# Spreading the triangular-solve level steps of a fused two-layer trunk over twelve half jobs instead of eight, with the gate, key and value jobs behind it reordered

## The chip, the cores and the metric

One core of a Trainium2 chip runs the whole program. The metric is the device time of one execution in microseconds, the median of three runs. TensorE multiplies; VectorE (DVE), ScalarE (ACT) and GpSimd (POOL) do elementwise work; SyncE's queue (SP) issues the weight transfers.

## The reference, cut to what matters

For x of 256 tokens by 1024 channels, two layers of: an RMSNorm, one wide projection (q, k, v, z, decay and beta logits, latents, gates), a gated delta rule over chunks of 64, latent attention, gating, an output projection, and a feed-forward block.

```python
qkv_a = jax.nn.silu(_causal_conv(qkv_a, conv_w[l]))
lower = jnp.where(strict, kk, 0.0) + jnp.eye(CHUNK, dtype=kk.dtype)
sol = lax.linalg.triangular_solve(lower, rhs, left_side=True, lower=True, unit_diagonal=True)
...
o_a = _rms_norm(o_a, gdn_norm_w[l]) * jax.nn.silu(z_a.reshape(b, s, GDN_HEADS, GDN_DV))
y_a = o_a.reshape(b, s, GDN_HEADS * GDN_DV) @ w_branch_a[l]
...
h = gates[:, :, 0] * y_a + gates[:, :, 1] * y_b
x = x + _rms_norm(h @ w_out[l], post_mix_norm_w[l])
```

## The kernel before

**Jobs and pieces.** All large products are cut into jobs. A job yields 256 output channels by 256 tokens in one of three PSUM banks (job j uses bank j mod 3, and waits for the evacuation of job j - 3). Its weights come in pieces of 128 x 1024 floats. Each piece is loaded by one 512 KB transfer that SP issues, then ScalarE writes its rounded upper part (whi, line 1110 through split_hi) and VectorE the remainder (wlo, line 1455, split_lo), and TensorE forms three products for each pair of 128x128 blocks: whi by upper, whi by lower, wlo by upper activations (lines 610 to 612). A piece is 24 such matmuls ("dense products"), each with its own weight load. The ring holds four pieces, so a piece is split three pieces ahead, and never before the piece four back is used up. "kn" and "vt" jobs (keys and values projected up from the latent) use half a piece each, "uq" jobs (queries) one piece of 768 columns, most others two. ScalarE evacuates k, v, q, z, gate, kn, vt and uq jobs.

**The order.** There is no runtime scheduler. `schedule()` (lines 121 to 268) writes out one list, ORDER, of (step, number). Every engine walks the same list and does its part of each step, with semaphore waits between engines; so each engine's queue is in that order, and an engine that waits in a step holds up all steps behind it. "half" is a job's first piece, "job" the rest; "late" steps are put behind the next job. `jobs_of_a_layer()` (lines 67 to 85) numbers the pieces in the order of use, which is also the order in memory and of SP's transfers.

**The level steps.** The triangular systems are solved by doubling: four levels (blocks of 2, 4, 8, 16), each with lvP and lvV (lines 899 to 924). Each of the two is 64 tiny products of 32 rows, which run as 128 matmuls with 128 weight loads: two halves of 64 pairs, a "burst" each. lvP of a level waits for VectorE's transpose of the level before (lv_xt); VectorE multiplies its result by a mask into PBq (line 1693, lv_p_out); lvV waits for that; VectorE then subtracts it from Xq and transposes (lines 1699, 1701). In before, a step's first half stands ahead of half a job and its second half inside it, behind six dense products (k == 1 of that piece), through the table LEVEL_STEP and `second_part`; 18 dense products follow. The eight steps lie on the eight pieces of v 0, v 1, (gate 0), v 2 and v 3. At the fifth step (n == 4) one half of gate 0 comes ahead of the step, and its other half takes the second part:

```python
for n, (kind, part, i) in enumerate(between):
    if steps[n][0][0] in ("lvP", "lvV"):
        LEVEL_STEP[...] = steps[n][0]
    o.extend(steps[n])
    part(kind, i)
    o.extend(behind[n])
```

**Behind the levels.** pairP, pairV, lastP, lastV, and t_v0, t_st, t_ks, t_v1 finish the solve and the chunk recurrence, one in front of each half of the q jobs. conv and silu (lines 1567, 1248) are the causal convolution on VectorE, six instructions a job, and its SiLU on ScalarE. Then come the kn jobs, qk 0 and 1 (TensorE at 878, evacuated by VectorE at 1672), kr (the shared rotary key: TensorE 851, VectorE 1623 to 1634), t_o (outputs of the delta rule: TensorE 1007, copied to oT by ScalarE 1371), the vt jobs and the uq jobs. ScalarE's evacuation of vt 0 waits for kr_out (line 1238), because the buffers overlap. t_o half h waits for qk_out 2 + 2h.

**The output norms.** For pair i of heads: osq i is a Square of oT on ScalarE (line 1281), then POOL adds the scaled square of q (line 1919, signal on_sq); onrm i is a product with a matrix of ones on TensorE that waits for on_sq i + 1 (lines 1019 to 1025, signal on_mm), then Ln and Exp on ScalarE (lines 1125 and 1127), a multiplication on VectorE (1723); osplit applies z on POOL and splits. In before, the rounds of the uq loop are: uq 4, osq 1; uq 5, (rope), onrm 0, osq 2; uq 0, (rope), onrm 1, osq 3; uq 1, onrm 2; uq 2, onrm 3; uq 3; then the attention scores sc 0. osq 0 is ahead of uq 4.

Of the kernel before, what the change touches and what calls it, by code (L numbers as in the profile page):

```python
# [66 lines left out]
def jobs_of_a_layer():  # L67


    jobs, n = [], 0  # L70
    for kind, numbers, pieces in (("lat", range(3), 2), ("k", range(1), 2), ("z", range(1), 2), ("k", range(1, 4), 2),
                                  ("z", range(1, 4), 2), ("v", range(2), 2), ("gate", range(1), 2), ("v", range(2, 4), 2),
                                  ("q", range(4), 2),
                                  ("kn", range(4), 0.5), ("vt", range(4), 0.5), ("uq", (4, 5, 0, 1, 2, 3), 1),
                                  ("gate", range(1, 8), 2), ("ya", range(4), 2), ("yb", range(4), 2),
                                  ("out", range(4), 2), ("ff1", range(16), 2), ("ff2", range(4), 8)):
        for i in numbers:
            jobs.append((kind, i, list(range(int(n), max(int(n) + 1, int(n + pieces))))))
            n += pieces
    for j, (kind, i, pieces) in enumerate(jobs):  # L80
        if kind in ("lat", "ff1") and i == 0:
            p = pieces[0]
            jobs[j] = (kind, 0, [p, p + 2])
            jobs[j + 1] = (kind, 1, [p + 1, p + 3])
    return jobs, int(n)
# [35 lines left out]
def schedule():  # L121
# [49 lines left out]
    half("z", 3)  # L171
    job("z", 3)

    between = [(kind, part, i) for kind in "vq" for i in range(4) for part in (half, job)]
    behind = {n: [] for n in range(len(between) + 3)}
    for n in range(8):
        behind[2 * n + 2].append(("conv", 4 + n))
        behind[2 * n + 3].append(("silu", 4 + n))
    for i in range(4):
        behind[2 * i + 5].append(("zsilu", i))  # L180
    behind[0].append(("latm", 0))
# [7 lines left out]
    steps = [[(step, lv)] for lv in range(len(SIZES)) for step in ("lvP", "lvV")]  # L189
    steps += [[(step, 0)] for step in ("pairP", "pairV", "lastP", "lastV")]  # L190
    steps += [[(step, 0), (step, 1)] for step in ("t_v0", "t_st", "t_ks", "t_v1")]
    for n, (kind, part, i) in enumerate(between):
        if steps[n][0][0] in ("lvP", "lvV"):
            LEVEL_STEP[JOBS[JOB["gate", 0]][2][1] if n == 4 else JOBS[JOB[kind, i]][2][n % 2]] = steps[n][0]
        if n == 4:
            half("gate", 0)
        o.extend(steps[n])
        if n == 4:
            job("gate", 0)
        part(kind, i)  # L200
        o.extend(behind[n])
    job("kn", 0)
    o += behind[16] + [("q2", 0)]
    job("kn", 1)
    o += [("qk", 0), ("qk", 1), ("qd", 0), ("kr", 0)]
    job("kn", 2)
    o += behind[17]
    job("kn", 3)
    o += [("q2", 1), ("q2", 2), ("q2", 3), ("lnexp", 1), ("t_o", 0)]
    job("vt", 0)  # L210
    o += [("qk", 2), ("qk", 3), ("qd", 1)]
    job("vt", 1)
    job("vt", 2)
    o.append(("t_o", 1))
    job("vt", 3)
    o.append(("osq", 0))
    for n, i in enumerate((4, 5, 0, 1, 2, 3)):
        job("uq", i)
        if i >= 4:
            late.append(("qrope", i - 4))  # L220
        if 1 <= n <= 4:
            o.append(("onrm", n - 1))
        if n < 3:
            o.append(("osq", n + 1))
    o += [("exptanh", 0), ("sc", 0), ("osplit", 0), ("osplit", 1)]
    for n in range(6):
        job("gate", 1 + n)
# [47 lines left out]
def build(nc, x_in, pos_in, w_in, prm_in, cst_in, out):  # L275
    with ExitStack() as ctx:
# [291 lines left out]
        def _(pe):  # L568
# [356 lines left out]

            def second_part(l, n, k):

                if n in LEVEL_STEP and k == 1:
                    step, lv = LEVEL_STEP[n]
                    (lvP_part if step == "lvP" else lvV_part)(l, lv, (2, 3))  # L930

            def pairP(l, _):
# [165 lines left out]
                      sc=sc, tr=tr, pv=pv, ysum=ysum, qrope=qrope)  # L1098
            for l in range(DEPTH):
                for what, n in ORDER:  # L1100
                    if what in do:
                        do[what](l, n)


# [945 lines left out]
```

How the kernel before makes its waits and increments, by code:

```python
        @block.sync  # L543
        def _(sp):
            def x_part(c):
                sp.dma_start(xT[:, 2 * c:2 * c + 2, :], x_in[:, 2 * c:2 * c + 2, :]).then_inc(s_x[c], 16)
            for n in range(DEPTH * NPIECE):
                if n == 2:
                    x_part(2)
                    x_part(3)
                elif n < 2:
                    x_part(n)
                sp.wait_ge(lo_ready, n + 1)
                sp.dma_start(raw[n % RING][:], w_in[n]).then_inc(loaded[n % RING], 16)
                if n == RING - 1:
                    sp.dma_start(cst[:, 0:C_FREQ], cst_in[:, 0:C_FREQ]).then_inc(s_in, 16)
                    sp.dma_start(pos_i[:], pos_in).then_inc(s_tab, 16)
                    sp.dma_start(cst[:, C_FREQ:NCST], cst_in[:, C_FREQ:NCST]).then_inc(s_tab, 16)
            for c in range(4):
                pair = slice(2 * c, 2 * c + 2)
                sp.wait_ge(x_done, due(DEPTH, x_done, 2 * c + 2))
                sp.dma_start(out[:, pair, :], xT[:, pair, :]).then_inc(s_out, 16)
            sp.wait_ge(s_out, 4 * 16)
# [2 lines left out]
        @block.tensor  # L567
        def _(pe):
            mm = nc.tensor.matmul
            pe.sem_inc(steps_done, RING)
            pe.wait_ge(s_warm, 1)
            for _n in range(8):
                mm(side[4][:, 0:S], sq[0][:, 0:P], sq[0][:, 0:S], start=True, stop=True)
# [9 lines left out]
            def piece(l, n):  # L584
                pe.wait_ge(lo_ready, l * NPIECE + n + 1 + RING)
                return whi[n % RING], wlo[n % RING]
```

## Time and profile before

| what | value |
|---|---|
| time, median of 3 runs | 1038.16 us (1035.57 to 1040.65) |
| profiled execution, its own time | 1044.89 us |
| span of the profiled execution | 1043.1 us |
| mean granted TensorE clock | 0.992 |
| TensorE busy (matmul) | 98% of the span |
| VectorE, ScalarE, POOL busy | 70%, 54%, 10% |
| weights | 304 transfers of 512 KB, 3.9 us to landing |

A time in the trace counts from the start of the span. Layer 0's level steps lie at about 84 to 133 us, layer 1's at 598 to 649 us. In a timeline a row is one instruction or a run of like ones (x with their number), the bracket is the idle time ahead of it and what ended it; "issue" there means that the profile shows nothing that was waited for. A granted clock of 1.00 is 2.4 GHz and of 0.50 is 1.2 GHz.

### The profile page before, as it was taken

Reading aid. Unit: us, or ns where it says so; the run is one execution under the profiler, and the core shown is the slowest. Engines: PE = TensorE matmul, PEld = TensorE weight load, DVE = VectorE, ACT = ScalarE, POOL = GpSimd, SP = SyncE. Lnnn points to the kernel's source line nnn. Section 1 sums busy time; section 2 is a strip of 40 time slices with the busy share of each in tenths; the row PEclk is TensorE's granted clock in tenths of the full one; section 3 lists DMA queues with packets and bytes.
Section 4 is the critical chain, followed back from the end, with each engine's and each line's share of the span. In section 5 each row is a group of like instructions: output and inputs, shape, how many; then the busy total and the mean of one; then the engine's idle time right before and its main releaser. Section 6 shows DMA issues by size and latency. Waiting matters only on the chain.

```text
span 1043.1 us, 24322 instructions
## 1 busy us (share of the span) xinstructions
PE 1019.8 (98%) x10626; PEld 990.7 (95%) x10626; DVE 733.4 (70%) x1024; ACT 558.7 (54%) x791; POOL 100.0 (10%) x76
## 2 busy tenths in 40 slices
PE   9998999999999999999999989999999999999996
PEld 8998999899999999999999989998999999999995
DVE  7887568697576788654598665677865777885543
ACT  7675475746445544434466634767554445544441
POOL 0010001310000222100000100015000003221000
PEclk9999999999999999999999989999999999999998
DMA  8543433434565466666535444334356646666661
GB/s 293 163 138 127 122 98 109 122 125 166 174 188 178 136 202 190 202 198 188 179 112 172 121 124 124 104 120 126 100 181 183 185 137 188 197 189 200 197 182 41
DMA packets 45609, 163.86 MB, mean 157 GB/s; under 512 B 5184, under 2 KB 5440, under 8 KB 45504
## 3 DMA queue, kind: packets, MB, share of 16 engines
q1 hardware_dynamic: 45360, 162.16, 50.4%
q8 instruction: 84, 1.38, 0.5%
q14 instruction: 21, 0.17, 0.1%
q10 hardware_dynamic: 144, 0.15, 0.0%
HBM read 161.25 MB, written 1.05 MB: 156 GB/s over the span
## 4 chain that ended last, share of the span: by engine, by line
PE 88%; DVE 7%; issue 2%; ACT 2%; DMA 0%; SPq 0%; DVEq 0%; ACTq 0%
PE dense L610 23%; PE dense L611 22%; PE dense L612 22%; DVE wlo L1455 2%; PE sides L922 1%; PE sides L1075 1%; PE sides L1049 1%; PE sides L1050 1%; PE sides L910 1%; PE dense L593 1%; PE dense L594 1%; PE sides L594 1%; PE sides L593 1%; PE dense L595 1%; PE sides L595 1%
## 5 line engine op out<-in xcount | busy, mean ns | idle before, releaser
L1455 DVE TENSOR_TENSOR wlo<-raw,whi 128x1024 fp32r<-128x1024 f32 (+1 forms) x303 | 392.6, 1303 | 196.9 <-ACT whi L1110 196.4
L1110 ACT ACTIVATE whi<-raw 128x1024 fp32r<-128x1024 f32 (+2 forms) x305 | 316.0, 1044 | 222.3 <-PE dense L612 201.6
L610 PE MATMUL dense<-uh,whi 128*128 128x256 f32 x768 | 224.8, 293 | 2.7 <-DVE ul L1484 1.3
L611 PE MATMUL dense<-ul,whi 128*128 128x256 f32 x768 | 215.3, 280 | 0.0
L612 PE MATMUL dense<-uh,wlo 128*128 128x256 f32 x768 | 215.1, 280 | 0.0
L610 PEld LDWEIGHTS dense<-uh,whi 128*128 128x128 f32 x768 | 146.6, 191 | 5.1 <-DVE ul L1484 1.4
L611 PEld LDWEIGHTS dense<-ul,whi 128*128 128x128 f32 x768 | 146.0, 190 | 1.3 <-issue 1.0
L612 PEld LDWEIGHTS dense<-uh,wlo 128*128 128x128 f32 x768 | 146.0, 190 | 0.0
L610 PE MATMUL dense<-fuh,whi 128*128 128x256 f32 x512 | 142.8, 279 | 0.4 <-DVE ful L1827 0.4
L611 PE MATMUL dense<-ful,whi 128*128 128x256 f32 x512 | 141.9, 277 | 0.0
L612 PE MATMUL dense<-fuh,wlo 128*128 128x256 f32 x512 | 141.9, 277 | 0.0
L610 PE MATMUL dense<-fh,whi 128*128 128x256 f32 x384 | 106.0, 276 | 0.0
L611 PE MATMUL dense<-fl,whi 128*128 128x256 f32 x384 | 106.0, 276 | 0.0
L612 PE MATMUL dense<-fh,wlo 128*128 128x256 f32 x384 | 106.0, 276 | 0.0
L610 PEld LDWEIGHTS dense<-fuh,whi 128*128 128x128 f32 x512 | 96.2, 188 | 1.6 <-issue 1.1
L612 PEld LDWEIGHTS dense<-fuh,wlo 128*128 128x128 f32 x512 | 96.4, 188 | 0.0
L611 PEld LDWEIGHTS dense<-ful,whi 128*128 128x128 f32 x512 | 96.1, 188 | 0.1
L610 PEld LDWEIGHTS dense<-fh,whi 128*128 128x128 f32 x384 | 72.1, 188 | 0.0
L611 PEld LDWEIGHTS dense<-fl,whi 128*128 128x128 f32 x384 | 72.1, 188 | 0.0
L612 PEld LDWEIGHTS dense<-fh,wlo 128*128 128x128 f32 x384 | 72.1, 188 | 0.0
L1929 POOL TENSOR_TENSOR fr<-fr 128x512 f32<-128x512 f32 x32 | 44.9, 1405 | 118.5 <-DVE fr L1796 118.5
L1899 POOL TENSOR_TENSOR sq<-sq,sq 128x512 f32<-128x512 f32 x8 | 10.4, 1296 | 349.9 <-ACT sq L1246 349.9
(320 smaller groups left out, 2095.5 us busy)
## 6 DMA issues: line engine op xcount, KB each, us to landing
raw<-weights SPq DMA_DIRECT2D x304, 512.0 KB, 3.9
xT<-x_t SPq DMA_DIRECT2D x4, 256.0 KB, 5.3
out_t<-xT SPq DMA_DIRECT2D x4, 256.0 KB, 2.3
cst<-consts SPq DMA_DIRECT2D x1, 512.0 KB, 8.1
prm_all<-params ACTq DMA_DIRECT2D x1, 150.0 KB, 3.8
pos_i<-pos SPq DMA_DIRECT2D x1, 128.0 KB, 7.8
cst<-consts SPq DMA_DIRECT2D x1, 6.0 KB, 7.6
```

What stands on the lines that cost most here:

```text
L593: mm(o_, h_[:, ws], ahi[:, k0 + k, :], start=first and k == 0, stop=False, skip_group_check=True)
L594: mm(o_, h_[:, ws], alo[:, k0 + k, :], start=False, stop=False, skip_group_check=True)
L595: x_ = mm(o_, l_[:, ws], ahi[:, k0 + k, :], start=False, stop=last and k == 3, skip_group_check=True)
L610: mm(o_, h_[:, ws], ahi[:, k0 + k, :], start=is_first, stop=False, skip_group_check=True)
L611: mm(o_, h_[:, ws], alo[:, k0 + k, :], start=False, stop=False, skip_group_check=True)
L612: x_ = mm(o_, l_[:, ws], ahi[:, k0 + k, :], start=False, stop=is_last, skip_group_check=True)
L910: r = mm(side[e][rows, 16 * g:16 * (g + 1)], LT[rows, g, e, rows], evens(Xq[rows, e, g, :], SIZES[lv]), start=True, stop=True)
L922: r = mm(side[e][rows, 16 * g:16 * (g + 1)], XTq[rows, e, g, :], PBq[rows, e, g, 0:16], start=True, stop=True)
L1049: mm(o_, qn[:, h, qt * P:(qt + 1) * P], kn[:, h, 0:w], start=True, stop=False)
L1110: return A(o_, i_, ACT.Copy)
L1455: TT(wlo[s][:, 0:w], raw[s][:, 0:w], f32(whi[s][:, 0:w]), ALU.subtract).then_inc(lo_ready, 1)
L1929: G(fr[i % 4][:], fr[i % 4][:], fr[i % 4][:], ALU.mult).then_inc(f_sq, 1)
```

## The change

The level steps are laid over twelve half jobs, three to a level. lvP stands ahead of the first, with its second half inside it as before (mark 1 in LEVEL_STEP). lvV has mark 2: it is left out of TensorE's walk of ORDER, and issued inside the second half job's piece: its first half at k == 2, its second at k == 3. So 18 + 12 = 30 dense products follow lvP's second half, and 6 + 24 = 30 follow lvV's. The other engines meet lvV ahead of that second half job's remaining piece, as before. gate 0 moves behind the q jobs, and takes the place beside t_v0 and t_st; kn 0 and 1 go beside t_ks, kn 2 and 3 beside t_v1. Then come q2 0, vt 0, qk 0, qk 1, qd, kr, vt 1, q2 1 to 3, t_o 0, vt 2, qk 2, qk 3, vt 3, uq 4, t_o 1. The rounds of the uq loop become: uq 4, t_o 1; uq 5, (rope), osq 0; uq 0, (rope), onrm 0, osq 1; uq 1, onrm 1, osq 2; uq 2, onrm 2, osq 3; uq 3, onrm 3. No instruction that computes is added or removed.

```diff
--- before.py
+++ after.py
@@ -69,8 +69,7 @@
 
     jobs, n = [], 0
     for kind, numbers, pieces in (("lat", range(3), 2), ("k", range(1), 2), ("z", range(1), 2), ("k", range(1, 4), 2),
-                                  ("z", range(1, 4), 2), ("v", range(2), 2), ("gate", range(1), 2), ("v", range(2, 4), 2),
-                                  ("q", range(4), 2),
+                                  ("z", range(1, 4), 2), ("v", range(4), 2), ("q", range(4), 2), ("gate", range(1), 2),
                                   ("kn", range(4), 0.5), ("vt", range(4), 0.5), ("uq", (4, 5, 0, 1, 2, 3), 1),
                                   ("gate", range(1, 8), 2), ("ya", range(4), 2), ("yb", range(4), 2),
                                   ("out", range(4), 2), ("ff1", range(16), 2), ("ff2", range(4), 8)):
@@ -171,11 +170,14 @@
     half("z", 3)
     job("z", 3)
 
-    between = [(kind, part, i) for kind in "vq" for i in range(4) for part in (half, job)]
-    behind = {n: [] for n in range(len(between) + 3)}
+    units = [(kind, part, i) for kind in "vq" for i in range(4) for part in (half, job)]
+    units += [("gate", half, 0), ("gate", job, 0), ("kn", job, 0), ("kn", job, 2)]
+    shares = [2, 1] * 4 + [1] * 8
+    ready = {n: [] for n in range(len(units))}
+    behind = {n: [] for n in range(len(shares))}
     for n in range(8):
-        behind[2 * n + 2].append(("conv", 4 + n))
-        behind[2 * n + 3].append(("silu", 4 + n))
+        ready[2 * n + 2].append(("conv", 4 + n))
+        ready[2 * n + 3].append(("silu", 4 + n))
     for i in range(4):
         behind[2 * i + 5].append(("zsilu", i))
     behind[0].append(("latm", 0))
@@ -189,39 +191,42 @@
     steps = [[(step, lv)] for lv in range(len(SIZES)) for step in ("lvP", "lvV")]
     steps += [[(step, 0)] for step in ("pairP", "pairV", "lastP", "lastV")]
     steps += [[(step, 0), (step, 1)] for step in ("t_v0", "t_st", "t_ks", "t_v1")]
-    for n, (kind, part, i) in enumerate(between):
-        if steps[n][0][0] in ("lvP", "lvV"):
-            LEVEL_STEP[JOBS[JOB["gate", 0]][2][1] if n == 4 else JOBS[JOB[kind, i]][2][n % 2]] = steps[n][0]
-        if n == 4:
-            half("gate", 0)
-        o.extend(steps[n])
-        if n == 4:
-            job("gate", 0)
-        part(kind, i)
+    at_unit = 0
+    for n, share in enumerate(shares):
+        for at_ in range(share):
+            kind, part, i = units[at_unit]
+            piece = JOBS[JOB[kind, i]][2][int(part is job) if kind != "kn" else 0]
+            if at_ == 0 and not (n < 2 * len(SIZES) and n % 2):
+                o.extend(steps[n])
+                if n < 2 * len(SIZES):
+                    LEVEL_STEP[piece] = (*steps[n][0], 1)
+            elif at_ == 1:
+                o.extend(steps[n + 1])
+                LEVEL_STEP[piece] = (*steps[n + 1][0], 2)
+            part(kind, i)
+            if kind == "kn":
+                job(kind, i + 1)
+            o.extend(ready[at_unit])
+            at_unit += 1
         o.extend(behind[n])
-    job("kn", 0)
-    o += behind[16] + [("q2", 0)]
-    job("kn", 1)
+    o.append(("q2", 0))
+    job("vt", 0)
     o += [("qk", 0), ("qk", 1), ("qd", 0), ("kr", 0)]
-    job("kn", 2)
-    o += behind[17]
-    job("kn", 3)
+    job("vt", 1)
     o += [("q2", 1), ("q2", 2), ("q2", 3), ("lnexp", 1), ("t_o", 0)]
-    job("vt", 0)
+    job("vt", 2)
     o += [("qk", 2), ("qk", 3), ("qd", 1)]
-    job("vt", 1)
-    job("vt", 2)
-    o.append(("t_o", 1))
     job("vt", 3)
-    o.append(("osq", 0))
     for n, i in enumerate((4, 5, 0, 1, 2, 3)):
         job("uq", i)
         if i >= 4:
             late.append(("qrope", i - 4))
-        if 1 <= n <= 4:
-            o.append(("onrm", n - 1))
-        if n < 3:
-            o.append(("osq", n + 1))
+        if n == 0:
+            o.append(("t_o", 1))
+        if n >= 2:
+            o.append(("onrm", n - 2))
+        if 1 <= n < 5:
+            o.append(("osq", n - 1))
     o += [("exptanh", 0), ("sc", 0), ("osplit", 0), ("osplit", 1)]
     for n in range(6):
         job("gate", 1 + n)
@@ -925,8 +930,10 @@
 
             def second_part(l, n, k):
 
-                if n in LEVEL_STEP and k == 1:
-                    step, lv = LEVEL_STEP[n]
+                step, lv, at_ = LEVEL_STEP.get(n, (None, 0, 0))
+                if at_ == 2 and k == 2:
+                    (lvP if step == "lvP" else lvV)(l, lv)
+                if at_ and k == (at_ + 1 if at_ == 2 else 1):
                     (lvP_part if step == "lvP" else lvV_part)(l, lv, (2, 3))
 
             def pairP(l, _):
@@ -1098,7 +1105,7 @@
                       sc=sc, tr=tr, pv=pv, ysum=ysum, qrope=qrope)
             for l in range(DEPTH):
                 for what, n in ORDER:
-                    if what in do:
+                    if what in do and (what, n, 2) not in LEVEL_STEP.values():
                         do[what](l, n)
 
 
```

## Rows read from the trace of the kernel before

**Rows 1.** The page: busy time by engine, share of the span, instructions
```profile
PE 1019.8 (98%) x10626; PEld 990.7 (95%) x10626; DVE 733.4 (70%) x1024; ACT 558.7 (54%) x791; POOL 100.0 (10%) x76
```

**Rows 2.** Waits of TensorE over the whole span: us in total, times, longest
```profile
PE sides L922 <- issue: 3.6, 2, 2.2
PE sides L910 <- issue: 2.7, 4, 0.9
...
PE sides L922 <- DVE PBq L1693: 1.1, 1, 1.1
...
PE dense L610 <- issue: 1.0, 1, 1.0
```

**Rows 3.** Timeline of TensorE, layer 1: start us, us, instructions [idle <- releaser]
```profile
608.31 0.56 PE L910 MATMUL sides<-Xq,LT 32*32 32x16 f32 x45 [0.51 <-issue]
...
609.70 0.72 PE L910 MATMUL sides<-Xq,LT 32*32 32x16 f32 x64
...
612.95 0.28 PE L610 MATMUL dense<-uh,whi 128*128 128x256 f32 x1 [0.95 <-issue]
...
615.29 0.63 PE L922 MATMUL sides<-PBq,XTq 32*32 32x16 f32 x52
618.15 0.40 PE L922 MATMUL sides<-PBq,XTq 32*32 32x16 f32 x12 [2.24 <-issue]
```

**Rows 4.** The page's instruction queue, and that queue in 610:612
```profile
q8 instruction: 84, 1.38, 0.5%
...
q8 instruction: 1, 0.02, 2.8%
```

**Rows 5.** Timeline of TensorE, layer 0, its longest stop
```profile
103.65 0.24 PE L922 MATMUL sides<-PBq,XTq 32*32 32x16 f32 x4 [1.34 <-issue]
```

**Rows 6.** Timeline of TensorE, layer 0: burst, dense products, a wait
```profile
85.79 0.73 PE L910 MATMUL sides<-Xq,LT 32*32 32x16 f32 x64
86.44 0.39 PE L610 MATMUL dense<-uh,whi 128*128 128x256 f32 x1
...
87.02 0.28 PE L611 MATMUL dense<-ul,whi 128*128 128x256 f32 x1
...
88.50 0.28 PE L612 MATMUL dense<-uh,wlo 128*128 128x256 f32 x1
89.83 0.72 PE L922 MATMUL sides<-PBq,XTq 32*32 32x16 f32 x64 [1.06 <-DVE PBq L1693]
```

**Rows 7.** Stretches: busy us by engine, PEclk, DMA; dense products at low clock
```profile
105.00:106.00 1.00, 1.00 (x8) 1.00 (x7) 1.00 (x2) 0.00 (x0) 0.00 (x0) 0.53 0.08 16
...
622.00:623.80 1.80, 1.80 (x11) 1.80 (x10) 0.22 (x1) 1.07 (x3) 0.00 (x0) 0.50 0.68 257
...
619.28 0.41 PE L610 MATMUL dense<-uh,whi 128*128 128x256 f32 x1
...
622.27 0.41 PE L612 MATMUL dense<-uh,wlo 128*128 128x256 f32 x1
```

**Rows 8.** Timelines of VectorE and ScalarE around kr
```profile
179.91 1.19 DVE L1634 TENSOR_TENSOR krz<-krb,kra 64x256 f32<-64x256 f32 x2
...
181.27 1.28 ACT L1290 ACT_TABLE_LOAD   x1
```

**Rows 9.** Timeline of ScalarE between two output norms
```profile
201.37 0.69 ACT L1125 ACTIVATE rn<-sides,bias_cols 128x512 f32<-128x512 f32 x1 [0.68 <-PE sides L1025]
...
202.63 0.62 ACT L1281 ACTIVATE sq<-oT 128x512 f32<-128x512 f32 x1
```

**Rows 10.** Timeline of POOL: the add behind it
```profile
203.33 1.43 POOL L1919 TENSOR_TENSOR sq<-sq,q 128x512 f32<-128x512 f32 x1 [2.46 <-ACT sq L1281]
```

**Rows 11.** Timeline of TensorE, ones-products; the stretch 200 to 204
```profile
200.31 1.02 PE L1025 MATMUL sides<-sq,cst 128*128 128x512 f32 x2
...
203.23 1.02 PE L1025 MATMUL sides<-sq,cst 128*128 128x512 f32 x2
...
200.00:204.00 4.00, 4.00 (x25) 2.89 (x23) 3.73 (x5) 3.29 (x6) 1.54 (x2) 1.00 0.37 102
```

## The prediction

> **What bounds the kernel now.** I read, in this order, the page's busy times and clock row, the waits of TensorE, its timeline over the level steps, and the timelines of the engines around the output norms. TensorE is busy for 1019.8 of 1043.1 us and nothing else is near it [rows 1], so a microsecond counts only if TensorE stops, runs at the lower clock, or gets more work. The change adds and removes no arithmetic. What can change is therefore in TensorE's own idle time [rows 2]: 3.6 + 2.7 + 1.0 = 7.3 us at lines 922, 910 and 610 with "issue" as releaser (nothing that the profile shows), and 1.1 us for PBq of VectorE. All lie in the level steps.
>
> The stops follow instructions, not data. In layer 1 TensorE resumes at 608.31, 612.95 and 618.15, in two cases with a burst cut in two [rows 3]. Between the first and second are 45 pairs of weight load and matmul of the burst, 6 dense ones, 64 of the next burst and 12 dense ones: 127 pairs, 254 instructions. Between the second and third are 6 + 64 + 6 + 52 = 128 pairs, 256 instructions. The instruction queue moved 84 packets, 1.38 MB [rows 4], for 21252 loads and matmuls: 253 to a packet. One packet moved in 610 to 612, between the restarts at 608.31 and 612.95 [rows 4]. So I read "issue" as a wait for the next block of 256 instructions. A block took 612.95 - 608.31 = 4.6 us and 618.15 - 612.95 = 5.2 us to come; in layer 0 a stop of 1.34 us is of the same form [rows 5]. A burst of 64 pairs takes 86.44 - 85.79 = 0.65 us, a dense pair (88.50 - 87.02) / 13 = 0.114 us [rows 6]: bursts eat a block faster than it arrives.
>
> The two longest stops also bring the clock down. From about 105.0 to 108.4 us and about 617.1 to 623.9 us the granted clock is 0.50 (1.2 of 2.4 GHz), and a dense product takes (622.27 - 619.28) / 14 = 0.213 instead of 0.114 us [rows 7]; before each fall the engine had bursts and a stop of 1.34 or 2.24 us. Nearly half (1 - 0.114/0.213 = 0.47) of what the engine works at that clock is lost: 0.47 x 3.4 = 1.6 us and 0.47 x (623.8 - 618.15) = 2.6 us, together 4.2 us.
>
> **The change part by part.** (1) *Level steps.* Each still issues two bursts with six dense products between, but 30 instead of 18 follow. The work is the same; dense products come in from later. The wait of 1.06 us for PBq at 89.83 [rows 6] goes: 12 more products give VectorE 12 x 0.114 = 1.4 us. Minus 1.1 us.
>
> For the stops I carry the block edges through the new order. A level step is 2 x 128 + 2 x 36 = 328 instructions instead of 304; counted from the first level burst, edges lie near 146 + 256k in layer 1 (back from the stop 19 pairs into the third step's first burst) and near 163 + 256k in layer 0. With the durations above, the shortest blocks of before run 2.2, 2.2 and 3.5 us in layer 0 and 2.6, 2.8 and 3.5 us in layer 1. Afterwards they run 2.2, 3.6 and 4.2 us, and 2.7, 2.8 and 4.3 us; the rest are over 4.7 us. An edge can still fall so that one block holds both bursts. But each short block now follows one of 4.7 to 6 us, so its successor's refill is not asked for late as after a stop. I take 0.8 us for each of the four short blocks and 0.2 us over the rest of a layer: 3.6 us of the 7.3 us stay, 3.7 us go. Bounds: nothing stays; or each short block costs 5.2 - 2.2 = 3.0 us at one edge in each layer and the total stays at 7.3 us.
>
> *Clock.* With stops of about 1 us instead of 1.3 and 2.2 us, I let one fall in the two layers remain, at 0.6 of the mean price of 2.1 us: 1.3 us. Minus 2.9 us; bounds 4.2 us and nothing.
>
> VectorE must evacuate lvP of level 1 behind a weight split, a convolution, ktrans and two latent steps. By my count it is done up to 0.5 us late in each layer, mostly under the stop at the same place: zero, bound 1.0 us. Pair, last and t_ steps keep 24 dense products or two kn jobs between them. gate 0 and its pieces move in the same order for TensorE, the splits and SP's weight DMAs alike, so each piece is still split three pieces ahead; SP issues no more transfers and POOL none. zero for all of these.
>
> (2) *vt 0 before kr.* ScalarE's evacuation of vt 0 waits for kr_out; it used to stand behind kr, now in front of it. Queued behind it on ScalarE are vt 1, three q2 squares, a table load and the evacuation of t_o 0. VectorE's kr work ends about 3.4 us after qk 1, then 0.5 + 0.5 + 1.6 + 1.3 + 1.1 us follow (the table load and the kr work are in [rows 8]), then a split for vt 2 on both engines, and only then can VectorE evacuate qk 2 and 3: some 11.6 us after qk 1. TensorE gets to t_o 1, which waits for them, at 11.3 us (0.6 kr, 1.4 vt, 2.6 t_o, 1.4 vt, 1.7 qk, 1.4 vt, 2.1 uq). Plus 0.3 us per layer, 0.6 us; bounds 0 and 1.5 us.
>
> (3) *Output norms.* This is the costly term. Before, osq i+2 was issued behind onrm i, so the square for onrm i+1 was a round old. Now osq i+1 stands behind onrm i on ScalarE, and onrm i+1 comes on TensorE after just one uq job. The chain runs: ones-product of onrm i, Ln, Exp, Square of osq i+1, POOL's add of q2, next ones-product. In the trace such a product begins at 200.31; Ln at 201.37, Exp behind it, Square at 202.63 [rows 9]; POOL's add of 1.43 us at 203.33, so it ends at 204.76 [rows 10]. With about 0.1 us for the signal that is 4.55 us. TensorE's own period is 203.23 - 200.31 = 2.92 us [rows 11]. It would wait 4.55 - 2.92 = 1.6 us. A round with an add of 1.3 us would give 1.5 us, and a weight load behind the wait can add 0.2 us. Onrm 1, 2 and 3 are hit; onrm 0 has uq 0 and two rope products as cover. Three times 1.6 us in two layers is 9.6 us; bounds 6 x 1.3 = 8 and 6 x 1.9 = 11.4 us. Nothing downstream pays it back, because TensorE does not wait in the attention that follows. The softmax keeps its place: relative to onrm 3 both its inputs and the gate products that cover it come about 2 us earlier.
>
> **Sum**, against the profiled execution's 1044.89 us: - 1.1 - 3.7 - 2.9 + 0.6 + 9.6 = +2.5 us, 1047.4 us. That execution is 0.65% above the median of the three runs, 1038.16 us, so the forecast for the median is 1038.16 x 1047.4 / 1044.89 = 1040.7 us. About 0.5% (5.2 us) is what a measurement of this kernel can tell from no change.
>
> **A rule that speaks otherwise.** The Trainium skill (Runtime: NRT & Kernel Launch, Instruction fetch mechanics) has TensorE hold 2048 instructions, refilled in blocks of 256, with the cost of an edge mostly hidden. The block size agrees with this trace (253 to a packet); the hiding does not, since TensorE stopped within three blocks of the first burst. By the rule the 3.7 and 2.9 us would have no cause that spacing touches; the sum above goes by the rows.
>
> **The rivals.** *Forecast case, 0.55*: both effects act and nearly cancel. Its own range is the sum of bounds taken moderately, -3 to +7 us: 1035 to 1045 us.
>
> *Faster, 0.12*: the levels lose all their stops and falls (-1.1 - 7.3 - 4.2 = -12.6 us) and the norm chain costs its lower bound: -12.6 + 8 = -4.6 us; with the chain partly hidden as well, -7 us. That is 1031 to 1034 us. For it: every block is longer or better spaced. Against it: nothing in the rows hides the chain, and a 2.2 us block remains.
>
> *Slower, the clock falls among the norms, 0.18*: three waits of 1.6 us stand 4.5 us apart. In this stretch the granted clock is now 1.00 [rows 11]. If idle gaps of that density let it fall as a 1.34 us stop between bursts did, each layer pays one or two falls of 1.6 to 2.6 us: +2.5 + 2 x 2.1 to +2.5 + 4 x 2.1, so +6.7 to +11 us, 1045 to 1049 us. It decides once the mean clock from uq 5 to sc 0 is under about 0.85. For it: idle of a third of each round. Against: the products between the gaps are full-sized, and single stops of 1.06 and 0.9 us were not followed by a fall.
>
> *The change does not do what it says, 0.15*: "issue" does not come from spacing, and stops and falls stay as they are: -1.1 + 0.6 + 9.6 = +9.1 us, 1047 us. Against it: 254 and 256 instructions between stops. For it: two stops of before are as long as a whole block's run. By the skill's rule this is the outcome, at the same time.
>
> **How the numbers follow.** The forecast case splits, by its range and the 5.2 us, into 0.49 within 0.5%, 0.05 slower and 0.01 faster. The faster case gives 0.07 and 0.05 within. The clock case gives 0.15 slower and 0.03 within. The last gives 0.12 slower and 0.03 within. Together: faster 0.08, same 0.60, slower 0.32. The range goes from 1033 us (half of the faster case) to 1049 us.
>
> **What would show it.** Right: TensorE waits at the ones-product of onrm (line 1025 of before) for POOL's sq, 1.4 to 1.8 us, six times; no wait for PBq at lvV 0; "issue" idle at the level lines down to 3 or 4 us and the remaining stops 256 instructions apart; less time at 0.50 clock between 105 and 108 and between 617 and 624 us. Wrong: no POOL wait at onrm; or "issue" idle still above 6 us; or a lower clock between uq 5 and sc 0. A wait of TensorE for AT or kr_out near t_o 1 above 1.5 us would mean that I priced part 2 too low.

## The result, and the profile after

| what | before | after |
|---|---|---|
| median | 1039.35 us (1035.46 to 1045.97, 20 runs) | 1046.69 us (1044.71 to 1048.99, 20 runs) |
| ratio, 95% interval | | 1.0061 [1.0047, 1.0076] |
| profiled execution, its own time | 1044.89 us | 1046.53 us |
| its span, mean granted clock | 1043.1 us, 0.992 | 1044.7 us, 0.994 |

The change makes the kernel slower by 0.61% (0.71% if the two medians are divided), just beyond the 0.5% that the prediction took as its limit. The forecast was 1040.7 us, 0.24% over the median shown then. The range of 1033 to 1049 us holds the measured time; the 1035 to 1045 us of the forecast case by itself does not. The profiled execution of before was longer than 17 of the 20 runs, so the two spans differ by only 1.6 us where the medians differ by 7.3 us.

The page of after, busy time by engine (before: [rows 1]):

```profile
PE 1017.9 (97%) x10626; PEld 987.4 (95%) x10626; DVE 727.1 (70%) x1024; ACT 559.2 (54%) x791; POOL 96.5 (9%) x76
```

The work is the same; TensorE's share has gone down by a point. Its waits over the whole span, largest first, as us in total, times, longest (before: [rows 2]):

```profile
PE sides L1032 <- POOL sq L1926: 8.3, 6, 1.7
PE dense L616 <- issue: 1.7, 1, 1.7
PE sides L578 <- DVE sq L1872: 1.6, 1, 1.6
...
PE sides L915 <- issue: 1.3, 1, 1.3
...
PE sides L927 <- DVE PBq L1700: 0.4, 1, 0.4
```

Two things are seen. The stops called "issue" went from 7.3 us in seven pieces to 1.7 + 1.3 = 3.0 us in two, and the wait for PBq from 1.1 to 0.4 us. That is another wait than before's: the 1.1 us at lvV of level 0 is gone, and 0.4 us at lvV of level 1 in layer 1 is new. In their place stands a wait that before did not have at all: 8.3 us in six pieces at line 1032, the ones-product of the output norm, for POOL's add at line 1926. The chain behind one such wait, in layer 0: TensorE, ScalarE and POOL in 200 to 206 us (before: [rows 9 to 11]). Columns are start us, busy us, instruction, and in the bracket the idle time ahead with its releaser:

```profile
200.97 1.12 PE L1032 MATMUL sides<-sq,cst 128*128 128x512 f32 x2 [1.67 <-POOL sq L1926]
...
205.44 1.12 PE L1032 MATMUL sides<-sq,cst 128*128 128x512 f32 x2 [1.30 <-POOL sq L1926]
...
209.92 1.12 PE L1032 MATMUL sides<-sq,cst 128*128 128x512 f32 x2 [1.23 <-POOL sq L1926]
```

```profile
202.13 0.69 ACT L1132 ACTIVATE rn<-sides,bias_cols 128x512 f32<-128x512 f32 x1 [1.56 <-PE sides L1032]
202.85 0.63 ACT L1134 ACTIVATE rn<-rn 128x512 f32<-128x512 f32 x1
203.39 0.62 ACT L1288 ACTIVATE sq<-oT 128x512 f32<-128x512 f32 x1
```

```profile
204.08 1.31 POOL L1926 TENSOR_TENSOR sq<-sq,q 128x512 f32<-128x512 f32 x1 [3.17 <-ACT sq L1288]
```

It reads as a ring: product at 200.97, Ln 202.13, Exp 202.85, Square 203.39, the add from 204.08 to 205.39, next product 205.44. One turn takes 205.44 - 200.97 = 4.47 us, and 209.92 - 205.44 = 4.48 us. POOL's own bracket says the same from its side: it stands idle for 3.17 us until the Square comes. Layer 1 repeats it. From the first of the four ones-products of a layer (196.21) to the last (209.92) it takes 13.71 us. Three rounds of before, 2.92 and 2.98 us long, take 8.85 us. So the norms come out 4.9 us longer in each layer, 9.7 us in both, and not only by the 8.3 us that the waits' row shows.

The stops that are left, from TensorE's timeline (before: [rows 3, 5, 6]):

```profile
97.95 0.69 PE L915 MATMUL sides<-Xq,LT 32*32 32x16 f32 x61
99.91 0.23 PE L915 MATMUL sides<-Xq,LT 32*32 32x16 f32 x3 [1.27 <-issue]
...
617.81 0.72 PE L927 MATMUL sides<-PBq,XTq 32*32 32x16 f32 x64 [0.45 <-DVE PBq L1700]
...
631.72 0.73 PE L927 MATMUL sides<-PBq,XTq 32*32 32x16 f32 x64
632.38 0.39 PE L615 MATMUL dense<-uh,whi 128*128 128x256 f32 x1
634.51 0.37 PE L616 MATMUL dense<-ul,whi 128*128 128x256 f32 x1 [1.74 <-issue]
```

The first stands three pairs ahead of the end of a burst, the other one dense product behind one. From the first level burst of the layer to the first stop the trace has 463 pairs on TensorE (459 of bursts and dense products, 4 of the transpose of k that stands between two levels), 926 instructions; to the second, in layer 1, 963 pairs, 1926. The stops of before, counted in the same way, come at 670, 1180 and 2198 instructions in layer 0 and at 654, 908, 1164 and 2180 in layer 1. So both stops of after lie on the grid of before: 926 is 670 + 256, and 1926 is 1164 + 3 x 254. The prediction's edges, 163 + 3 x 256 = 931 and 146 + 7 x 256 = 1938, miss them by 5 and 12.

Stretches of after by engine (before: [rows 7, 11]); the last number but two is the granted clock:

```profile
101.00:105.00 4.00, 4.00 (x24) 4.00 (x23) 2.48 (x5) 2.32 (x4) 0.00 (x0) 0.57 0.03 11
...
197.00:214.00 17.00, 12.80 (x89) 10.71 (x88) 10.65 (x12) 12.41 (x18) 8.45 (x6) 1.00 0.38 123
...
634.00:638.00 4.00, 3.49 (x20) 3.49 (x20) 1.51 (x2) 2.23 (x5) 0.00 (x0) 0.59 0.44 135
```

Each of the two stops has a fall to half clock by it, of 3.4 us: in layer 0 it begins 1.4 us after TensorE has gone on, in layer 1 already in the stop, at 633.9. Before had one of 3.4 us and one of 6.8 us. Through the norms, where TensorE is busy for only 12.80 of 17 us, the clock stays at 1.00.

### The profile page after: what moved, and what is told of

The parts are those of the page before. It is cut to its first block, busy times and chain, and to the rows that moved or that the text cites. A ratio compares the mean times of both kernels' runs of the same rounds, so it can differ in the third digit from the quotient of the medians.

```text
span 1044.7 us, 24322 instructions
## 1 busy us (share of the span) xinstructions
PE 1017.9 (97%) x10626; PEld 987.4 (95%) x10626; DVE 727.1 (70%) x1024; ACT 559.2 (54%) x791; POOL 96.5 (9%) x76
## 3 DMA queue, kind: packets, MB, share of 16 engines
HBM read 161.25 MB, written 1.05 MB: 155 GB/s over the span
## 4 chain that ended last, share of the span: by engine, by line
PE 81%; issue 8%; DVE 7%; ACT 2%; POOL 1%; DMA 0%; SPq 0%; DVEq 0%; POOLq 0%; ACTq 0%
PE dense L615 22%; PE dense L616 21%; PE dense L617 21%; DVE wlo L1462 2%; POOL sq L1926 1%; PE sides L927 1%; PE sides L1082 1%; PE sides L1056 1%; PE sides L1057 1%; PE dense L598 1%; PE dense L599 1%; PE sides L598 1%; PE sides L599 1%; PE dense L600 1%; PE sides L600 1%
```

## The experiments

All are compared with the kernel before on the same chip. Three chips were used: experiments 1, 2, 4 and 5 with 11 runs of before (median 1040.85 us), 3, 7, 9 and 10 with 29 (1041.89), 6 and 8 with 23 (1040.37). Kernels of different chips, and after, whose ratio to before is 1.0061, are compared by their ratios. A kernel's lines have other numbers than after's by a few; the tiles are the same.

### 1. norms_back: after, without the change to the norm rounds

```diff
+    o.append(("osq", 0))
     for n, i in enumerate((4, 5, 0, 1, 2, 3)):
         ...
-        if n >= 2:
-            o.append(("onrm", n - 2))
-        if 1 <= n < 5:
-            o.append(("osq", n - 1))
+        if 1 <= n <= 4:
+            o.append(("onrm", n - 1))
+        if n < 3:
+            o.append(("osq", n + 1))
```

> The changed kernel with the rounds of the output norms as in before (osq 0 ahead of uq 4, then osq i+2 behind onrm i), all else of the change kept, t_o 1 still behind uq 4. Theory A (the norm chain is the loss): the six waits of TensorE for POOL at the ones-product, 8.3 us in the changed kernel's trace, are gone; the median falls by 8 to 9 us, to 1038 us, 0 to 2 us under before (ratio 0.998 to 1.000). Rival B (the loss sits in the level steps or in the moved gate, kn and vt jobs): the waits go, but the time stays 4 us or more above before (ratio 1.004 or more).

Measured: 1036.55 us (1035.25 to 1038.24, 6 runs) against 1040.85, ratio 0.9954 [0.9937, 0.9971]. TensorE no longer waits for POOL. By the ratios it is 1.0061 - 0.9954 = 1.07%, 11 us (give or take 2.3), below after, where 8 to 9 us were expected, and 0.46% below before, where 0 to 0.2% was: the level part by itself makes the kernel faster by more than I had said, and the norm rounds take more than it brings. Of after's two falls of the clock this profile has one, of 3.4 us in layer 1; in layer 0 a stop of 1.05 us at the place of after's has none. Its waits of TensorE:

```profile
PE sides L916 <- issue: 2.8, 2, 1.7
...
PE dense L616 <- issue: 0.8, 1, 0.8
```

### 2. norms_only: before, with only the norm rounds of after

Experiment 1's edit the other way round, in before.

> The kernel before with nothing changed but the rounds of the output norms, as the change has them (osq i+1 behind onrm i, one uq job ahead of the next ones-product). Theory A: six waits for POOL of 1.2 to 1.7 us, 8 to 9 us in all, and a time 8 to 9 us above before (ratio 1.008). Rival B: 0 to 3 us above before. If the clock falls among these waits (my third rival), more than 11 us above before and a granted clock under 0.9 between uq 5 and sc 0.

Measured: 1050.69 us (1046.28 to 1053.45, 5 runs), ratio 1.0093 [1.0071, 1.0114], 0.93% of 1040.85 or 9.7 us. So the norm rounds cost 11 us taken off after and 9.7 us put on before, which the intervals do not tell apart; within them the two parts of the change add up. Its waits and its level stops carry a second finding:

```profile
PE sides L1024 <- POOL sq L1918: 8.4, 6, 1.7
PE sides L909 <- issue: 2.2, 3, 1.0
...
PE sides L921 <- issue: 1.3, 2, 1.1
```

```profile
103.26 0.24 PE L921 MATMUL sides<-PBq,XTq 32*32 32x16 f32 x4 [1.06 <-issue]
...
616.03 0.63 PE L921 MATMUL sides<-PBq,XTq 32*32 32x16 f32 x52
616.94 0.30 PE L921 MATMUL sides<-PBq,XTq 32*32 32x16 f32 x12 [0.28 <-issue]
```

```profile
104.00:109.00 5.00, 5.00 (x59) 4.87 (x60) 2.50 (x3) 3.17 (x6) 0.00 (x0) 1.00 0.34 108
617.00:624.00 7.00, 7.00 (x127) 6.81 (x128) 4.56 (x8) 4.43 (x7) 0.00 (x0) 1.00 0.38 135
```

The order up to here is before's, and TensorE stops at the same instructions: ahead of the last 4 pairs of a burst in layer 0, and between pair 52 and 53 of one in layer 1. But the second stop takes 0.28 us where the profile of before had 2.24 us [rows 3], the level stops add up to 3.5 instead of 7.3 us, and the clock does not fall at all in the level steps of either layer. Where a stop can come is set by the order; whether it comes and how long it lasts differs from one execution to the next.

### 3. spacing_undone: norms_back, with the level steps again 6 and 18 apart

```diff
-    shares = [2, 1] * 4 + [1] * 8
+    shares = [1] * 16
...
-            if at_ == 0 and not (n < 2 * len(SIZES) and n % 2):
+            if at_ == 0:
...
+    half("gate", 0)
+    o.extend(ready[16])
+    job("gate", 0)
+    o.extend(ready[17])
+    for i in range(4):
+        job("kn", i)
```

> norms_back with the spacing of the level steps taken back: lvP and lvV each ahead of a half job, two bursts with six dense products between and 18 behind, on v 0 to v 3; gate 0 and all four kn jobs stand together behind q 3. The moved gate, key and value jobs stay moved. Theory A (the gain of norms_back over before is the spacing's): stops for instructions rise from 3.6 to 5 to 8 us over both layers, the wait of about 1 us for PBq at lvV 0 of layer 0 is back, and the time is 4 to 6 us above norms_back, within 0.2% of before. Rival (the gain comes from the moved jobs): within 1.5 us of norms_back.

Measured: 1041.83 us (12 runs) against 1041.89, ratio 0.9995 [0.9981, 1.001]. The gain of norms_back is gone, 0.41% or 4.3 us, with gate 0, the kn and the vt jobs still behind the q jobs. The last steps of the solve and the t_ steps go back beside the q jobs together with the spacing, so the run by itself does not part the two; the trace does, since nothing waits there. It has the stops of before again, 3.6 + 2.7 + 1.0 us (in ten pieces), the wait of 1.1 us for PBq, and a fall of 3.4 us in each layer. So it is the spacing that brings the gain.

### 4. shift64: after, with 64 more instructions ahead of level 0's first burst

```diff
             def lvP_part(l, lv, gs):
...
+                if lv == 0:
+                    for b, g, e, rows in quads((0,)):
+                        mm(side[e][rows, 16 * g:16 * (g + 1)], LT[rows, g, e, rows], evens(Xq[rows, e, g, :], SIZES[lv]),
+                           start=True, stop=True)
```

> The changed kernel with 16 of the tiny products of level step 0 issued twice (same operands, same values written again): 64 more instructions ahead of the level steps in each layer, 0.3 us of work each. Theory C (block edges every 256 instructions): the stops move with the edges, 64 instructions earlier in the level steps of layer 0 and 128 in layer 1. The stop of 1.27 us three pairs before the end of lvP's second burst of level 1 in layer 0, and the one of 1.74 us one product behind lvV's second burst of level 2 in layer 1, are gone from there; in layer 1 a stop may come at the last pairs of lvV's second burst of level 3. Rival E (stops belong to a place in the work, by data or by a buffer): they stay at the same two products.

Measured: 1051.86 us in one run, which says little of the time; the place of the stops was the question. Two of them in the timeline:

```profile
91.73 0.73 PE L931 MATMUL sides<-PBq,XTq 32*32 32x16 f32 x64
...
93.09 0.28 PE L617 MATMUL dense<-uh,wlo 128*128 128x256 f32 x1
96.16 0.58 PE L615 MATMUL dense<-uh,whi 128*128 128x256 f32 x1 [2.80 <-issue]
...
648.64 0.64 PE L931 MATMUL sides<-PBq,XTq 32*32 32x16 f32 x55
650.67 0.25 PE L931 MATMUL sides<-PBq,XTq 32*32 32x16 f32 x9 [1.39 <-issue]
```

Both stops of after are gone from their places. One now stands six dense products behind lvV of level 0, in layer 0, and one after 55 of the 64 pairs in the last lvV of layer 1. No data dependence was touched there. Counted with the extra instructions, the stops of layer 0 now come at 672 and 1944, and before's grid has an edge at 670 and one at 670 + 5 x 255 = 1945. The one in layer 1 comes at 2626, which is 64 (the extra instructions of layer 0) below 1164 + 6 x 254 = 2688, within 2. The stops go with the count of instructions, and with 64 more of them one came out at 2.80 us, longer than any in before.

The transfers name the cause. The instruction queue of [rows 4] moves its packets one by one, and in the traces of all twelve kernels 47 stops called "issue" of 0.25 us or more lie in the level steps. Most of these packets took 0.9 to 1.3 us, one took 2.2 us, and every one of the stops ends 1.1 to 1.6 us after its packet has ended. Take the stop of 2.24 us in before and of 0.28 us in norms_only. The packet ahead of it begins at 615.74 in before and at 614.62 in norms_only, and TensorE goes on 2.41 and 2.32 us later. Counted from the first level burst of the layer, the packet begins at 17.7 us in before and at 14.0 us in norms_only, while TensorE comes to the edge at 17.8 and 16.0 us. So the stop is short where the packet comes early.

### 5. whole_bursts: norms_back, with each level step as one burst of 128 pairs

```diff
-                lvP_part(l, lv, (0, 1))
+                lvP_part(l, lv, (0, 1, 2, 3))
...
-                lvV_part(l, lv, (0, 1))
+                lvV_part(l, lv, (0, 1, 2, 3))
...
-                if at_ and k == (at_ + 1 if at_ == 2 else 1):
-                    (lvP_part if step == "lvP" else lvV_part)(l, lv, (2, 3))
```

> As norms_back, but each level step issues its 128 pairs of weight load and matmul in one burst instead of two of 64 with six dense products between; 36 dense products follow. Theory C (a stop comes where 256 instructions run out faster than the next block of 256 arrives, 3.6 to 5.2 us): a burst of 128 pairs is a block by itself and runs in 1.3 us, so stops grow, from about 3 us in two layers to 6 to 8 us, with one or two more falls of the clock of about 1.6 us each; against it sixteen fewer changes between burst and dense product at 0.3 us save 4.8 us. Sum against norms_back: -1 to +4 us. Rival D (the stops have nothing to do with how densely instructions come): stops stay at about 3 us, and it is 4 to 5 us faster than norms_back.

Measured: 1034.45 us (1032.73 to 1037.88, 6 runs), ratio 0.9934 [0.9914, 0.9953]. I had expected it no better than norms_back by more than 1 us, and 6 to 8 us of stops; it came out 2.1 us lower, with 4.1 us of stops. The two intervals overlap, so what is shown is that cutting the bursts brings nothing with this spacing. Two of its four stops:

```profile
95.96 1.26 PE L916 MATMUL sides<-Xq,LT 32*32 32x16 f32 x128
99.54 0.58 PE L616 MATMUL dense<-uh,whi 128*128 128x256 f32 x1 [1.77 <-issue]
...
605.06 1.21 PE L916 MATMUL sides<-Xq,LT 32*32 32x16 f32 x122
608.02 0.30 PE L916 MATMUL sides<-Xq,LT 32*32 32x16 f32 x6 [1.75 <-issue]
```

### 6. whole_unspaced: spacing_undone, with whole bursts

Experiment 5's edit in spacing_undone.

> spacing_undone (the step spacing of before) with each level step as one burst of 128 pairs ahead of its half job. Theory A (the idle time follows how many instructions run in how much time over two or three blocks, not how the tiny ones are grouped inside a step): issue stops of 6 to 9 us in all, within 2 us of spacing_undone's 7.3, the wait for PBq down from 1.05 to about 0.4 us, time within 3 us of spacing_undone. Theory B (cutting the bursts is what keeps a block from draining at once, a burst of 256 instructions in 1.3 us against a refill of over 4 us): stops of 12 us or more and 4 to 9 us over spacing_undone, ratio to the kernel before 1.004 or more.

Measured: 1040.0 us (1037.56 to 1043.35, 12 runs) against 1040.37, ratio 0.9996 [0.9978, 1.0014], the ratio of spacing_undone. Stops: 2.3 + 1.8 + 1.0 + 0.6 = 5.7 us, below the 6 to 9 us that I had expected. The wait for PBq went up to 1.9 us instead of down to 0.4. VectorE's queue shows why:

```profile
87.15 2.36 DVE L1467 TENSOR_TENSOR wlo<-raw,whi 128x1024 fp32r<-128x1024 f32 x2 [1.89 <-ACT whi L1122]
89.43 0.42 DVE L1705 TENSOR_TENSOR PBq<-sides,cst 128x256 f32<-128x256 f32 x1
```

VectorE multiplies into PBq only behind two weight splits, which end at the same time whatever lvP does; TensorE comes to lvV earlier and waits longer for the same moment, 89.99 us. At the old spacing too, halves or wholes make no difference. That speaks for a stop that comes from the density of instructions over several blocks, and against one that a single dense burst makes; it was argued from sums and not tried further.

### 7. even_bursts: norms_back, with 18 dense products behind every burst

```diff
             elif at_ == 1:
-                o.extend(steps[n + 1])
                 LEVEL_STEP[piece] = (*steps[n + 1][0], 2)
+            elif n < 2 * len(SIZES):
+                LEVEL_STEP[piece] = (*steps[n][0], 3)
...
             o.extend(ready[at_unit])
+            if at_ == 1:
+                o.extend(steps[n + 1])
...
-                if at_ and k == (at_ + 1 if at_ == 2 else 1):
+                if k == {1: 3, 3: 1}.get(at_):
```

> norms_back with the four bursts of a level spread evenly, 18 dense products behind each, instead of 6 and 30. Theory C (a block of 256 instructions must run longer than the next takes to come): the shortest block then runs 3.6 us instead of 2.2, so stops fall from 3.6 us to under 1.5 us over both layers and at most one fall of the clock is left; lvV again has just 18 products behind lvP, so one wait of about 1 us for PBq may come back. Sum: 2 to 6 us faster than norms_back. Rival D (stops do not depend on density): same as norms_back or slower by the wait for PBq.

Measured: 1044.45 us (12 runs) against 1041.89, ratio 1.003 [1.0016, 1.0043]. The stops did as the blocks let expect: one of 0.28 us was left. But the kernel is 0.8% over norms_back by the ratios, where 2 to 6 us less was expected. Its waits, and VectorE's queue ahead of the first of them:

```profile
PE sides L919 <- DVE XTq L1712: 8.0, 2, 4.0
PE sides L931 <- DVE PBq L1704: 2.1, 2, 1.1
```

```profile
108.77 1.23 DVE L1466 TENSOR_TENSOR wlo<-raw,whi 128x1024 fp32r<-128x1024 f32 x1 [2.88 <-ACT whi L1121]
109.91 2.44 DVE L1589 SCALAR_TENSOR_TENSOR vT<-cb,prm_all,vT 128x255 f32<-128x255 f32 x6
112.28 0.41 DVE L1710 TENSOR_TENSOR Xq<-Xq,sides 128x256 f32<-128x256 f32 x1
112.72 0.71 DVE L1712 STREAM_TRANSPOSE XTq<-Xq 128x512 f32<-128x512 f32 x1
```

In spreading the bursts I had put lvV's evacuation behind the second half job on VectorE too. There it waits for a split and a convolution, and TensorE stands for 4.0 us, twice. Around the end of each of these waits the clock falls too, for 3.4 us in layer 0 and 6.8 us in layer 1, as much as in the profile of before with its 7.3 us of stops.

### 8. even_vector_first: even_bursts, with lvV's evacuation back ahead of that half job

```diff
             elif at_ == 1:
+                o.extend(steps[n + 1])
                 LEVEL_STEP[piece] = (*steps[n + 1][0], 2)
...
             o.extend(ready[at_unit])
-            if at_ == 1:
-                o.extend(steps[n + 1])
```

> even_bursts with VectorE's part of lvV (and ScalarE's) put back ahead of the second half job's split and convolution; TensorE's order is the same as in even_bursts. Theory V (the two waits of 4.0 us for XTq come from VectorE's own queue, where a split and a convolution of 2.4 us stand ahead of lvV's subtraction and transpose): these waits go to under 0.5 us each, the stops at instruction blocks stay under 1 us in all, waits for PBq of 1.06 us may stay; so 7 to 9 us less than even_bursts, 1035 to 1038 us where the kernel before has about 1040, ratio 0.995 to 0.998. Rival (TensorE asks too early whatever VectorE's order, because only 18 dense products, 2.05 us, lie between lvV's second burst and lvP's first): the XTq waits stay above 1.5 us, at all three level changes, and the time stays at 1040 us or more.

Measured: 1040.3 us (12 runs) against 1040.37, ratio 0.9993 [0.9975, 1.0012]. The XTq waits are gone altogether, so they did come from VectorE's order. The time missed the range of 1035 to 1038 us: it is 0.37% or 3.9 us less than even_bursts, not 7 to 9, because the next wait in line took up half of what went:

```profile
PE sides L930 <- DVE PBq L1703: 4.4, 2, 2.2
PE sides L930 <- issue: 1.7, 2, 1.0
```

lvP now ends 18 dense products (2.05 us) ahead of lvV instead of 30, and at level 1 VectorE comes to PBq only behind a split, a convolution, ktrans and two latent steps. A fall of 3.4 us follows each of the two waits. With issue stops of 2.1 us in all (another of 0.4 us at a dense product) it has 1.5 us less of them than norms_back, and 4.4 us more waits for PBq. The change's uneven spacing, 6 and 30, is better than an even one (0.9954 against 0.9993, intervals apart), and the waits say why: the 30 cover VectorE's queue.

### 9. kr_first: norms_back, with vt 0 behind kr again

```diff
-    o.append(("q2", 0))
+    o += [("q2", 0), ("qk", 0), ("qk", 1), ("qd", 0), ("kr", 0)]
     job("vt", 0)
-    o += [("qk", 0), ("qk", 1), ("qd", 0), ("kr", 0)]
```

> norms_back with qk 0, qk 1, qd 0 and kr ahead of vt 0, as in before, so that ScalarE no longer stands for kr_out in the evacuation of vt 0 (4.4 us in each layer of the changed kernel). Theory A (that wait of ScalarE is covered; TensorE shows no wait near t_o 1): within 1 us of norms_back. Rival (my prediction's term of 0.3 us a layer, or more than the trace shows): 0.6 to 1.5 us faster than norms_back.

Measured: 1035.96 us (6 runs), ratio 0.9944 [0.9924, 0.9964], against norms_back's 0.9954. No difference shows, but a term of 0.6 us is smaller than these intervals tell. The trace decides: in after, ScalarE's evacuation of vt 0 does wait for kr, for 4.4 us in each layer, and TensorE never stops for it:

```profile
ACT vt L1117 <- DVE krz L1641: 8.8, 2, 4.4
```

### 10. add_on_vector: after, with the norm's add on VectorE

```diff
+            def osq(l, i):
+                ...
+                TT(sq[i % 2][:], sq[i % 2][:], q2[:, pair, :].rearrange("p c s -> p (c s)"), ALU.add).then_inc(on_sq, 1)
...
-            def osq(l, i):
-                ...
-                G(sq[i % 2][:], sq[i % 2][:], q2[:, pair, :].rearrange("p c s -> p (c s)"), ALU.add).then_inc(on_sq, 1)
```

> The changed kernel with the add behind osq (Square plus q2) on VectorE instead of POOL, nothing else moved. Theory A (TensorE waits for the chain ones-product, Ln, Exp, Square, add): the add takes 0.7 instead of 1.3 us but stands behind VectorE's own multiplication of the same round, so each of the six waits shrinks by 0.3 to 0.7 us, from 1.4 to about 0.9 us; 2 to 4 us faster than the changed kernel, 1043 to 1045 us. Rival (the waits belong to something else that POOL's record only coincides with): waits of 1.4 us stay.

Measured: 1043.61 us (12 runs), ratio 1.0019 [1.0003, 1.0035], by the ratios 0.42% or 4.4 us under after. The wait and the add:

```profile
PE sides L1032 <- DVE sq L1731: 4.6, 6, 0.9
```

```profile
203.00 0.68 DVE L1731 TENSOR_TENSOR sq<-sq,q 128x512 f32<-128x512 f32 x1
```

The link takes 0.68 instead of 1.31 us, and each wait falls by about 0.6 us (8.3 - 4.6 = 3.7 us over six). So the chain's length is what TensorE pays, link by link; a faster link shortens the wait, and of what was tried only a round more between the steps removes it. In this profile the level stops add up to 3.6 + 0.7 us, with two of 1.70 and 1.95 us, and yet the clock is 1.00 in both layers' level steps:

```profile
85.00:135.00 50.00, 47.88 (x1264) 45.09 (x1265) 36.74 (x62) 28.13 (x44) 0.00 (x0) 1.00 0.46 141
598.00:655.00 57.00, 54.31 (x1456) 51.22 (x1455) 40.39 (x67) 31.26 (x49) 0.00 (x0) 1.00 0.43 134
```

## Why the prediction was nearly right, and what it mis-sized

| step | forecast | measured |
|---|---|---|
| wait for PBq | 1.1 us gone | 1.1 us gone, another of 0.4 us new |
| issue stops | 7.3 to 3.6 us | 7.3 to 3.0 us |
| clock falls | 4.2 to 1.3 us | at the prediction's price 4.2 to 2.9 us (half clock 10.2 to 6.8 us) |
| vt 0 before kr | +0.6 us | 0 in the trace |
| norm chain | +9.6 us | waits 8.3 us, rounds 9.7 us; runs 9.7 and 11 us |
| against the profiled execution | 1047.4 us | 1046.53 us |
| against the median | 1040.7 us | 1046.69 us |
| ratio to before | 1.0024 | 1.0061 |

**The norm chain** was right in mechanism, place and size. The turn was forecast at 4.55 us and measured at 4.47; what TensorE does in it takes 4.47 - 1.30 = 3.17 us instead of 2.92. So the row shows 1.30 us in place of 1.6, and 1.67 us at the first one, whose add took 1.69 us. By the rounds it is 9.7 / 6 = 1.6 us for each of the six, and the runs have 1.6 to 1.9 us. I read the difference to the row as the weight load behind the wait, which the prediction had named with 0.2 us: the loads' own row has 9.5 us of idle where the products' has 8.3.

**The stops** were right in cause: shift64 moved them by their count, each ends at the same distance behind an instruction packet, spacing_undone brought them back, norms_back took about half away. **The clock** is the step that the rows bear out least. It was to give back 2.9 us and gave 1.3: TensorE worked 3.4 and 2.8 us at half clock, 0.47 x 6.2 = 2.9 us. A fall stayed in each layer instead of one in the two, though norms_back, with the same spacing, had just one; and its cause was put too simply, since 1.70 and 1.95 us of stop had no fall in add_on_vector where 1.27 us had one in after.

**The wait for PBq** at level 1 was named and set to nothing; it is the 0.4 us that after has. **vt 0 before kr** was given a small cost and has none that shows. The wait on ScalarE is there, but TensorE's work ahead of t_o 1 covers it.

**The step that was off** is the use of one profiled execution as if it were the typical one. The sum took -1.1 - 3.7 - 2.9 us from the profiled execution of before and scaled the result to the median, as if every execution of before had 7.3 us of stops and 10.2 us at half clock. It had not: in norms_only the same level order had 3.5 us of stops and no fall, in spacing_undone 7.3 us of stops and 6.8 us at half clock. The runs say it as well. The profiled execution took 1044.89 us at a mean granted clock of 0.992; of the 23 runs of before on the third chip the three at 0.991 average 1045.5 us and the two at 0.997 average 1037.7 us, with 0.994 in the middle. So the level part was credited with 7.7 us, or 7.1 us with the 0.6 us of vt 0, 0.68%, and it brings 0.46% [0.29, 0.63], 4.8 us (norms_back). The cost of the norms stays whole. The forecast's ratio of 1.0024 falls 0.37%, 3.8 us, short of 1.0061: 2.3 us are the levels and the other 1.5 us the norms, if norms_back is taken for both. Against the median it is 6.0 us; another 1.2 us are the median of before, 1039.35 us over 20 runs instead of 1038.16 over three, and 1.0 us lies between the ratio of the runs and that of the medians.

**What was luck.** Against the profiled execution the same sum comes to 1047.4 us, 0.9 us from what after's profile has. The terms do not add up as well as that. With what the rows measured they are -0.7 - 4.3 - 1.3 + 0 + 9.7 = +3.4 us, and the two executions differ by 1.6 us; for the other 1.8 us no row was found. And 1046.69 us lies in the range only because the range went up to 1049 us for the third and the fourth case, neither of which came. The class given 0.60, within 0.5%, did not come either; slower had 0.32.

**The rivals.** *Faster* is out: two stops and two falls stay, and nothing hides the chain. *The clock falls among the norms* is out, with 1.00 over 197 to 214 us. *The change does not do what it says* is out as a cause, though 1047 us was its time: norms_back is faster than before by 0.46%, spacing_undone is not. What was said for it, that two stops of before are as long as a whole block's run, holds for one: 2.24 us against 2.2; the next is 1.34 us. The Trainium skill (Runtime: NRT & Kernel Launch, Instruction fetch mechanics) would have given that outcome, since it has the cost of a block's edge mostly hidden. The block of 256 agrees with the runs, whose stops lie 254 to 256 instructions apart or multiples of that, in shift64 too; the hiding holds for the rest of the kernel, but not here, where an edge cost up to 2.80 us.

**What stays open.** Why the packet ahead of the same stop begins 5.2 us after the one before it in before and 4.0 us in norms_only, and with it the 2.24 or 0.28 us of the stop, was not tried. Nor does any run show what decides whether the clock falls by a stop. Nor is it settled whether whole bursts are better than halves, or only no worse. The best kernel of the study is whole_bursts, 0.9934 [0.9914, 0.9953] of before, 1.27% or 13 us under after.

## What to carry to other kernels

When a change takes away stops that differ from run to run, don't sum against one profiled execution and scale: its excess over the median may be those stops. Compare its time and mean granted clock with those of the other runs first. When two steps of a ring over three engines come one round closer together, add up the whole ring (here 4.5 us) and compare it with the round of the engine that bounds the kernel (here 2.9 us in before); the difference is paid in every round and in every run. When an order is spread for one engine, look at where the other engines' parts of the step went: in even_bursts that cost 8 us of waits where the spreading saved 3 us of stops.

## What the runs showed of the hardware that I had not expected

- A stop between instruction blocks has a fixed place and no fixed length: the same instruction of the same order waited 2.24 us in before, 1.68 us in spacing_undone and 0.28 us in norms_only. Its place is a count of TensorE's matmuls and weight loads, 254 to 256 from edge to edge; before, after, norms_only, spacing_undone and shift64 share one grid within a few instructions.
- TensorE goes on 1.1 to 1.6 us after the packet of the instruction queue has ended, in all 47 stops of 0.25 us or more.
- One burst of 128 pairs in 1.26 us, 256 instructions, costs no more than two of 64: 0.9996 against 0.9995 at the old spacing, 0.9934 against 0.9954 at the new.
- A fall of the clock to 0.50 does not go by the length of the stop before it alone: 1.70 and 1.95 us of stop left it at 1.00 (add_on_vector), one of 1.27 us did not (after). Waits of 1.2 to 1.7 us between full-sized products, three in 9 us, left it at 1.00 as well.
